# A two-layer diffusion trunk: expert results summed in PSUM, and slot rows read in one piece and transposed by VectorE

## The reference, cut to what matters

```python
comb = jnp.sum(jax.nn.one_hot(eidx, N_EXPERTS) * wsel[..., None], axis=1)
hg = jnp.einsum('td,edf->tef', t, w_gate)
hu = jnp.einsum('td,edf->tef', t, w_up)
act = jax.nn.silu(hg) * hu * comb[:, :, None]
y = jnp.einsum('tef,efd->td', act, w_down)
x = layer_norm(ALPHA * x + g2 * y, ln_w, ln_b)
```

## Time and profile before

| | us |
|---|---|
| median of 3 runs | 1203.97 (1202.0 to 1207.95) |
| the profiled execution | 1201.09 |
| its span | 1199.4 |
| mixture stage of layer 0, first gate matmul to last down | 332.3 to 574.7 |
| first hyena matmul | 613.9 |
| mixture stage of layer 1 | 905.0 to 1164.4 |

### The profile page before, as it was taken

One profiled execution on the slowest core, in us unless ns is written; L12 is line 12 of the kernel. 1 busy time (PEld: TensorE's weight loads), 2 busy tenths in 40 slices (PEclk: granted clock), 3 DMA queues, 4 the chain that ended last, 5 costly groups with the idle time before them and its releaser, 6 DMA issues.

```text
span 1199.4 us, 24149 instructions
## 1 busy us (share of the span) xinstructions
PE 1013.1 (84%) x9499; PEld 561.7 (47%) x9499; DVE 400.3 (33%) x1149; ACT 239.8 (20%) x507; POOL 190.9 (16%) x389
## 2 busy tenths in 40 slices
PE   4899998899769899795679999999978977998564
PEld 2344447654435455453345555455454544555231
DVE  0320115744612222121353533645552221222116
ACT  0401003631411121111131111210141121121102
POOL 0320000300032222122110001002004221222111
PEclk9999999899789999898889999999979998999988
DMA  8998232977589999999892314636765799899984
GB/s 354 324 343 299 95 126 97 350 298 317 222 302 396 388 407 393 397 399 394 305 377 99 140 71 143 243 123 241 292 256 211 270 391 408 337 395 393 394 349 158
DMA packets 76278, 344.62 MB, mean 287 GB/s; under 512 B 8883, under 2 KB 9011, under 8 KB 62900
## 3 DMA queue, kind: packets, MB, share of 16 engines
q1 hardware_dynamic: 54756, 291.40, 62.9%
q0 software_dynamic: 14512, 41.78, 10.2%
q10 hardware_dynamic: 6944, 10.49, 2.5%
HBM read 320.02 MB, written 23.63 MB: 287 GB/s over the span
## 4 chain that ended last, share of the span: by engine, by line
PE 63%; DMA 21%; DVE 10%; ACT 2%; issue 2%; SPq 1%; POOL 0%; POOLq 0%; ACTq 0%; DVEq 0%
PE bank L954 13%; PE bank L743 12%; PE bank L1019 11%; PE bank L961 7%; DMA ring<-in_moe_w_up_dram 7%; PE bank L872 7%; DMA ring<-in_ada_w_dram 3%; DMA ring<-in_moe_w_down_dram 3%; DMA arena<-in_moe_w_up_dram 3%; PE bank L633 3%; DMA ring<-in_ev_w_in_dram 3%; PE bank L1122 1%; PE bank L1098 1%; ACT arena L1409 1%; DVE arena L1531 1%
## 5 line engine op out<-in xcount | busy, mean ns | idle before, releaser
L954 PE MATMUL bank<-ring,arena 128*32 128x256 f32 x2496 | 149.9, 391 | 28.8 <-DMA ring<-in_moe_w_up_dram 25.7
L743 PE MATMUL bank<-ring,arena 128*128 128x512 f32 x336 | 146.7, 598 | 2.5 <-DMA ring<-in_ev_w_in_dram 2.5
L954 PE MATMUL bank<-arena 128*32 128x256 f32 x1792 | 108.1, 395 | 28.3 <-DMA arena<-in_moe_w_up_dram 28.3
L1019 PE MATMUL bank<-arena,ring 128*128 128x384 f32 x384 | 126.3, 492 | 1.9 <-issue 1.9
L1529 DVE TENSOR_TENSOR arena<-arena,bank 128x64 f32<-128x64 f32 x136 | 27.4, 201 | 296.2 <-ACT arena L1409 296.2
L954 PEld LDWEIGHTS bank<-ring,arena 128*32 128x32 f32 x2496 | 83.7, 113 | 88.5 <-issue 41.7
L961 PE MATMUL bank<-ring,arena 128*32 128x256 f32 x1440 | 87.0, 382 | 27.3 <-DVE arena L1531 22.2
L743 PEld LDWEIGHTS bank<-ring,arena 128*128 128x128 f32 x336 | 64.2, 192 | 82.9 <-issue 80.2
L1019 PEld LDWEIGHTS bank<-arena,ring 128*128 128x128 f32 x384 | 73.5, 192 | 54.4 <-issue 5.0
L954 PEld LDWEIGHTS bank<-arena 128*32 128x32 f32 x1792 | 60.3, 114 | 72.0 <-issue 39.4
L872 PE MATMUL bank<-ring,arena 128*128 128x512 f32 x192 | 83.2, 593 | 1.3 <-DVE arena L2096 1.3
(11 more groups left out here) (367 smaller groups left out, 1074.9 us busy)
## 6 DMA issues: line engine op xcount, KB each, us to landing
ring<-in_ada_w_dram SPq DMA_DIRECT2D x24, 2048.0 KB, 13.4
ring<-in_moe_w_down_dram SPq DMA_DIRECT2D x20, 2048.0 KB, 23.5
ring<-in_moe_w_gate_dram SPq DMA_DIRECT2D x18, 2048.0 KB, 24.1
ring<-in_moe_w_up_dram SPq DMA_DIRECT2D x18, 2048.0 KB, 29.4
arena<-in_moe_w_gate_dram SPq DMA_DIRECT2D x14, 2048.0 KB, 26.7
arena<-in_moe_w_up_dram SPq DMA_DIRECT2D x14, 2048.0 KB, 31.9
arena<-in_moe_w_down_dram SPq DMA_DIRECT2D x12, 2048.0 KB, 20.1
ring<-in_ev_w_in_dram SPq DMA_DIRECT2D x7, 2048.0 KB, 19.4
```

The source lines that it names most:

```text
L743: last = pe.matmul(bank[3 * (c % 2) + t], hT[:, k, t * P:(t + 1) * P], slot8(n)[:, k, :], start=k == 0, stop=k == KT - 1)
L954: last = pe.matmul(bank[1][q * BLK:(q + 1) * BLK, 0:HALF], slot_inT[:, k, :], both[:, :, k, q * P:(q + 1) * P], start=k == 0, stop=k == KT ...
L1019: last = pe.matmul(bank[c % 3][:, 0:T], slot8(n)[:, k, (c % 4) * P:(c % 4 + 1) * P], hT[:, k, :], start=k == 0, stop=k == KT - 1)
```

## The change

**Results.** `slot_out` is now 128 partitions by 256: each quarter of the partitions holds a quarter of the 1024 columns for the block's 32 slots. Nothing is stored to DRAM, gathered or joined. Six PSUM banks (`joined`) hold the sums of all 384 tokens through the stage. They are opened with matmuls that write zeros (`begin_sums`). In each block `add_to_tokens` adds the block before it with 12 matmuls: weights are 32 partitions of `sel_w` by 128 tokens, moving data is 32 partitions of `slot_out` by 256 columns, in three groups of four that use the four 32-row groups of the array. `sel_w` holds the router weight where a token owns the slot. VectorE makes it per block from `token_slot` and `token_w`, which TensorE (`along_tokens`) and ScalarE spread over the partitions before the stage. The third group waits until the first has ended. Gate and up stop before their last step until the former block's results and selection are there.

**Rows.** Only block 0 is picked, by 24 matmuls with `h_tok` as weights, directly in channel layout. A block is read as one 128 KB DMA, 4 KB on each of 32 partitions. GpSimd's copy puts it into another order, and VectorE transposes it in four 32x256 pieces. TensorE no longer transposes rows. ScalarE writes `h_tok` unpermuted.

**Around it.** The idle matmuls (`WARM`, `pe_last`) and the scaled identities are gone. Hyena weights wait for no gather. After layer 0, the modulation columns are computed after the totals, and TensorE waits for all three totals before it transposes.

```diff
-            for c in range(WARM):
-                pe.matmul(bank[3], ident, h_tok[:, c % NT, 0:512], start=True, stop=True)
+            pe.wait_ge(weights_rdy, l + 1)
+            for r in range(2):
+                last = along_tokens(bank[1 + r], lambda t: wsel[:, r, t:t + 1])
+            last.then_inc(spread_mm, 1)
+            for b in bank[3:]:
+                begin_sums(b)
...
-            for t in range(NT):
-                for q in range(4):
-                    block, h = divmod(q, 2)
-                    last = pe.matmul(bank[2][q * BLK:(q + 1) * BLK, :], pick[:, t, block * BLK:(block + 1) * BLK],
-                                     h_tok[:, t, h * 512:(h + 1) * 512], start=t == 0, stop=t == NT - 1)
+            for k in range(KT):
+                for t in range(NT):
+                    last = pe.matmul(bank[0][:, k * BLK:(k + 1) * BLK], h_tok[:, t, :].rearrange("p (c k) -> p k c", k=KT)[:, k, :],
+                                     pick[:, t, :], start=t == 0, stop=t == NT - 1)
...
+            def add_to_tokens(turn, closing=False):
+                for t in range(NT):
+                    if t == 2:
+                        pe.wait_ge(S["first_added"], turn)
+                        pe.sem_inc(passed, 1)
+                    for q in range(4):
+                        rows = slice(q * BLK, (q + 1) * BLK)
+                        half = NT * q + t
+                        last = pe.matmul(joined[:, t, q, :], sel_w[rows, t * P:(t + 1) * P], slot_out[rows, :], start=False,
+                                         stop=closing and t > (half ^ 1) % NT)
+                    if t == 0:
+                        last.then_inc(S["first_added"], 1)
+                return last
...
                 for k in range(KT):
+                    if k == KT - 1:
+                        pe.wait_ge(S["evac_dve"], b + 1)
+                        pe.wait_ge(S["evac_act"], b + 1)
+                        pe.wait_ge(S["sel"], b + 1)
                     last = gate_and_up(s, k)
                 last.then_inc(S["gu_mm"], 1)
-                rows_to_channels()
+                add_to_tokens(b + 1)
                 pe.wait_ge(S["act"], b * 2 + 1)
-                pe.wait_ge(S["evac_dve"], b + 1)
-                pe.wait_ge(S["evac_act"], b + 1)
...
+                    pool.tensor_copy(slot_in.rearrange("s (g k i) -> s g k i", g=4, k=KT),
+                                     slot_ahead[k].rearrange("s (g i k) -> s g k i", g=4, k=KT)).then_inc(S["row_rdy"], 1)
+                    pool.wait_ge(S["row_rdy"], pair * 2 + (k + 1))
+                    rows_ahead(pair * 2 + (k + 3), k)
...
-                    for h in range(2):
-                        act.dma_start(slots[bass.ds((pair * 2 + odd) * BLK, BLK), h * 512:(h + 1) * 512],
-                                      slot_out[odd][h * BLK:(h + 1) * BLK, :]).then_inc(S[f"stored{odd}"], 16)
...
+                dve.wait_ge(S["row_rdy"], b + 1)
+                rows_to_channels()
+                dve.wait_ge(S["down_mm"], b + 1)
+                dve.tensor_copy(slot_out[0:2 * BLK, :], bank[1][0:2 * BLK, 0:HALF]).then_inc(S["evac_dve"], 1)
+                for r, o in enumerate((sel_w, sel_w1)):
+                    last = dve.scalar_tensor_tensor(o, token_slot[:, r, :], block_slot, token_w[:, r, :], ALU.is_equal, ALU.mult)
+                last.then_inc(S["sel_step"], 1)
+                dve.wait_ge(S["sel_step"], b * 2 + 1)
+                dve.tensor_tensor(sel_w, sel_w, sel_w1, ALU.add).then_inc(S["sel"], 1)
```

More of the change, by code:

```diff
@@ L385, in trunk_program @@
         idle = tiny(1)
+        block_slot = tiny(1)
+        rows_over = tiny(2)
         warm = tiny(1)
@@ L429, in trunk_program @@
         lnrow_in = sem("lnrow_in")
-        gathered = [sem(f"gathered{t}") for t in range(NT)]
         out_done = sem("out_done")
@@ L569, in pool_moe @@
-            rows_ahead(2, 0)
-            rows_ahead(3, 1)
-            with pool.Fori(1, pairs) as pair:
-                for odd in range(2):
-                    pool.wait_ge(S[f"row_in{odd}"], pair * 32)
-                    pool.wait_ge(S["rowT_mm"], pair * 2 + (odd + 1))
-                    pool.tensor_tensor(idle, wsel[:, 0, 0:1], wsel[:, 0, 0:1], ALU.add)
-                    pool.tensor_copy(slot_in, slot_ahead[odd]).then_inc(S["row_rdy"], 1)
-                    pool.wait_ge(S["row_rdy"], pair * 2 + (odd + 1))
-                    rows_ahead(pair * 2 + (odd + 2), odd)
@@ new lines, in pool_moe @@
+            with pool.Fori(0, pairs) as pair:
+                for k in range(2):
+                    pool.wait_ge(S[f"row_in{k}"], pair * 16 + 16)
+                    pool.wait_ge(S["rowT"], pair * 2 + (k + 1))
+                    pool.tensor_tensor(idle[0:BLK, :], eps_col[0:BLK, :], eps_col[0:BLK, :], ALU.add)
+                    pool.tensor_copy(slot_in.rearrange("s (g k i) -> s g k i", g=4, k=KT),
+                                     slot_ahead[k].rearrange("s (g i k) -> s g k i", g=4, k=KT)).then_inc(S["row_rdy"], 1)
+                    pool.wait_ge(S["row_rdy"], pair * 2 + (k + 1))
+                    rows_ahead(pair * 2 + (k + 3), k)
@@ L584, in pool_moe @@
             if l == 0:
+                pool.wait_ge(S["down_mm"], before_last)
+                pool.tensor_tensor(idle[0:BLK, :], eps_col[0:BLK, :], eps_col[0:BLK, :], ALU.add).then_inc(pool_chain, 1)
+                pool.wait_ge(pool_chain, 2)
                 norm_gate_rows(pool)
-            for odd in range(2):
-                pool.wait_ge(S[f"row_in{odd}"], pairs * 32)
-            pool.wait_ge(S["stored0"], stores * 32 + 32)
-            pool.wait_ge(S["stored1"], odd_stores * 32 + 32)
@@ L590, in pool_moe @@
-            pool.wait_ge(S["rowT"], blocks + 1)
-            pool.tensor_tensor(idle, wsel[:, 0, 0:1], wsel[:, 0, 0:1], ALU.add).then_inc(pool_chain, 1)
-            pool.wait_ge(pool_chain, 2 * l + 3)
-            for t in range(NT):
-                for r in range(2):
-                    pool.indirect_dma_start(picked[:, t, r, :], None, slots[:, :],
-                                            bass.IndirectOffsetOnAxis(ap=idx[:, r * NT + t:r * NT + t + 1], axis=0)).then_inc(gathered[t], 16)
+            for k in range(2):
+                pool.wait_ge(S[f"row_in{k}"], pairs * 16 + 16)
@@ L1419, in act_moe @@
[L1419 to L1425 removed]
+                act.activation(h_tok[:, u // 2, u % 2 * 512:u % 2 * 512 + 512], bank[u], ACT.Copy).then_inc(htok_act, 1)
+            act.wait_ge(spread_mm, 2 * l + 1)
+            for r in range(2):
+                last = act.activation(token_w[:, r, :], bank[1 + r][:, 0:T], ACT.Copy)
```

296 lines of the change are left out of this document (126 added, 170 removed).

## The result

| | before | after |
|---|---|---|
| median | 1205.96 us (4 runs, 1202.0 to 1208.93) | 1232.93 us (4 runs, 1231.77 to 1235.46) |
| span of the profiled execution | 1199.4 | 1230.7 |
| mixture of layer 0, first gate matmul to end of last down | 332.3 to 574.7 | 341.8 to 598.6 |
| first hyena matmul | 613.9 | 633.9 |
| mixture of layer 1, the same | 905.0 to 1164.4 | 935.2 to 1205.9 |

The account below looks back on a forecast made before the run. The mixture was taken as bound by weight transfers, with TensorE some 30 us a layer behind as slack. Terms -19.7 + 4.9 - 9.6 = -24.4 took 1201.09 to 1176.7, median 1179; range 1160 to 1209.

Parts of the forecast that it names:

- The period, TensorE's side: Mixture blocks: six waves of additions on four row groups side by side add 0.6 us, period 6.92 instead of 6.32.
- three quarters: Rival on the additions: four row groups give 3.07 times one's speed; period +0.39 us, +18, 1197 us; chance 0.16.
- The period, VectorE's side: Mixture blocks: VectorE's 3.3 us of added work and GpSimd's copy, doubled to 1.2, lie beside TensorE's 6.92 at no cost.
- a rival with 0.13: Late selection: VectorE's passes can't run beside GpSimd's copy, selection 1.0 us late each block; +46, 1225 us; chance 0.13.
- The slack of the selection: Before gate's last step in each block: selection ready at 6.2, weights load at about 6.45, slack 0.25 us.
- VectorE's own durations: Added work per block: four transposes at 0.38 each, two passes over 384 columns 0.6, a sum 0.54; 3.3 us.
- Lead-in: Before each mixture: spread, zeroing and 48 pick records (5.7 us) delay gate to 336.8 from 332.28, layer 1 by 4.8 us.
- The bound of +11: Upper bound of the lead-in's delay, for weights that load at half pace; the lower bound was +2.
- Behind layer 0: Stores, gathers, joins and hyena weights' wait go; modulation is late next; hyena stage at 594.2 instead of 613.92, -19.7 us.
- The queue gives its time back: Without stores, ScalarE's DMA queue returns 12.7 us a layer, 0.375 a block, where transfers bound.
- End of layer 1: Behind the last down: 12.8 us to the total become 4.2, and totals no longer wait for joins; -9.6 us.
- Layer 1: Mixture: lead-in and longer blocks delay held loads by 9.6, 14 blocks without stores return 5.3, last block 0.6; +4.9 us.

Follow-up runs that it names:

- experiment 1: Changed kernel with GpSimd's row copy waiting for the selection instead of the row transposes: median 1206.42 us, 1.0039 times the kernel before.
- experiment 2: Changed kernel with tokens written in channel order, so the pick's weights have unit stride and GpSimd's copy moves runs of 32: 1196.18 us.
- three_repairs: Changed kernel with copy behind the selection, tokens in channel order and gate rows on ScalarE's queue: median 1188.18 us, 0.9836 times the kernel before.
- experiment 5: Changed kernel with VectorE's two passes reading one SBUF tensor each, every router weight counted as 0.5: 1221.65 us.
- experiment 3: Changed kernel with the norm's gate row loads issued by ScalarE's queue before the last expert, not by GpSimd behind its loop: 1229.78 us.
- experiment 9: `three_repairs` without earlier gate rows, with shorter lead-in and layer 1's stores put back unread: layer 1's last gate 261.9 us after its first, against 255.6 without stores.

## Why the prediction was wrong

The forecast had a span of 1175.0 (1199.4 less 24.4). Measured are 1230.7, 55.7 more. The lengths of the stretches are those of the kernel before with the forecast's terms in them; for the mixture of layer 1 that is 259.4 + 4.9 - 4.8, since the 4.8 of lead-in stand in the row above it:

| stretch | forecast | measured | difference |
|---|---|---|---|
| to the end of the last down of layer 0 | 568.6 | 598.6 | +30.0 |
| from there to the hyena stage | 25.6 | 35.3 | +9.7 |
| hyena stage to the first gate of layer 1 | 295.9 | 301.3 | +5.4 |
| mixture of layer 1 | 259.5 | 270.6 | +11.1 |
| end | 25.4 | 24.9 | -0.5 |

- **The period, TensorE's side: right.** I took 6.92, and it is 6.86 as soon as nothing holds it. All four row groups ran side by side, their six waves in one block of 24 records in 1.61 us. Gate's last wave to down is 0.54 us longer than before, where I had 0.6 with the wait. By the three quarters of the Trainium skill (page "TensorE: Matmul & The Clock Gate", Part 3, "Measured speedup vs the span model") the additions would have cost 0.39 us more; the runs don't show it for this shape (behind the change of shape the waves start 0.22 us apart), and that rival falls.
- **The period, VectorE's side: the step that failed.** "It lies beside TensorE's 6.92, at no cost while the selection is ready", with "doubles to 1.2, and lies beside it too" for GpSimd's copy. The copy took 2.07, since it steps over eight elements, and it holds VectorE's passes. Without one of the two the step would have stood (experiments 1 and 2). Together they cost 0.86 us a period beyond 6.92: some 27 of the 30 us of layer 0 against the forecast (31 periods), and 6 of the 11 of layer 1, by the difference to `three_repairs` (264.3). Repairing them gave back less, 22.0 us in layer 0 (experiment 1). I had this as a rival with 0.13, named the place, and priced it at 1225, with 1.0 us a block and 4.6 us per 0.1. The runs gave 0.86 beyond my period, and in experiment 1 26.3 us of span for 0.92 us of period, 2.9 per 0.1. That the kernel still came out above 1225 is the work of two other misses, the pick and the gate rows below. What I counted against it, transposes that ran undisturbed beside the copy, was true of 128x64 transposes and said nothing of passes, which are held.
- **The slack of the selection: small by 0.2 us.** I had it at 0.25 us, and it was about 0.4: the first pass was held by some 1.35 us (1.96 in most blocks, against 0.61), the period by 0.92. The two shorter passes of experiment 5 add 0.4 to the slack, and its period is 0.52 above 6.86. The 0.3 of hold in experiment 2 cost nothing.
- **VectorE's own durations:** two passes 0.62 each (0.6 taken), the transposes 0.435 (0.38), the sum 0.56 (0.54). Near enough for the sum, but the transposes make the second bound of 6.79.
- **Lead-in: mechanism right, one term mis-sized.** 48 records of the pick were priced at the pace of 24 transposes with unit stride. They took 0.24 each instead of 0.118, 5.8 us a layer. In layer 0 the first gate came 5.0 us later than forecast and block 1 2.6 later (349.6 instead of 347.0). It did not wait for rows read back, as the forecast had it; it followed block 0 after 7.84 us, at the period of the others. With all three repairs it comes at 345.0, 4.6 us earlier, and there it does wait for its rows, by 0.8 us. Layer 1 paid for the pick nearly in full (its first gate came 5.4 us later than forecast against the hyena stage). The bound of +11 held it (9.5 measured in layer 0).
- **Behind layer 0: a cover missed.** "Stores, gathers, joins and the wait in front of the hyena weights go" was right. Asked what is late next, I named the modulation. The gate rows' loads stand on GpSimd behind its row loop, and I put them at nothing. The change moved the loop's last copy behind the last block's row transposes, and with it these loads from 17.6 us before the last down's end to 3.9 us behind it. They cost 8.0 us (experiment 3). With them repaired, the hyena stage starts 26.9 us after the last down, where I had 25.6.
- **The queue gives its time back: right** in experiment 9, but behind an engine that had become the bound it was worth little: DMA share 0.89 and 0.84 in the changed kernel.
- **End of layer 1: right.** 4.2 us from down to the total, and 10.1 gained against 9.6.
- **Layer 1: a rest that is only placed.** Even with all repairs its mixture takes 264.3 us and not 259.5. Up to the first held load it goes as forecast (issued 36.5 us after the first gate; 33.5 before and 3.0 for five longer blocks). The load at 1048.49 before is this one in `three_repairs`:

```profile
1043.02 0.33 SPq L507 DMA_DIRECT2D ring<-in_moe_w_down_dram  x1
```

It comes 149.4 us after the first gate, against 143.5 before and 4.8 forecast, so 1.2 too late. From there to the end of the last down the stage takes 114.9 us against 115.9 before: 1.0 less, where I had 4.7 less (5.3 from the queue and the last block's 0.6). The remaining 3.7 us lie there. This load landed 10.0 us after its issue (7.6 before), and the last block took 9.6 us (8.6 before). Why is open. Experiment 9 says that the stores themselves cost 4.0 in that stretch, so something else took back what the queue gave.

With the three misses cured, the kernel comes near the forecast: 1188 against 1179 in the median, 1184.2 against 1175.0 in the span, half of the difference in layer 1. It is faster than before by 1.6% (1.0 to 2.3), where the forecast had 2.1%.

## What to carry to other kernels

Before work is laid beside other work "at no cost", ask for each pair of instructions that will lie over one another whether the two engines can run at once in exactly these forms. One form that ran undisturbed (a transpose) says nothing of another (a pass over SBUF). Two lateness terms that are harmless alone (a copy of twice the length, and passes that wait for a copy) can add up past the slack, here about 0.4 us, and then the whole of the excess is paid in every period.

Take prices from rows of the same stride: a copy on GpSimd and a weight load of TensorE both doubled with a stride of eight floats. And when a step of a loop is moved behind another wait, look at what the same engine issues behind the loop: it moves as well.

## What the runs showed of the hardware

- GpSimd's copy of 1024 floats on 32 partitions: 1.03 us in runs of 32, 2.07 with a stride of eight. While it runs, VectorE's pass with two SBUF tensors (0.62 alone) and its pass with one (0.41 alone) last until about its end, up to 1.98 and 1.79 us. A copy out of PSUM (0.42), a product with one factor in PSUM (0.18 to 0.22), and transposes of 128x64 in 32x32 pieces (0.24) keep their times.
- Float32 weight loads of 128x128 with a stride of 32 bytes: one matmul each 0.24 us at either level of the granted clock, against 0.12 with unit stride. In layer 1 the profile shows TensorE 100% busy in the pick, and still the granted clock fell from 1.00 to 0.50 during it.
- Four row groups of the array with 32 rows each kept the pace of four column groups, 0.22 us a wave: six waves and the change of shape behind them took 1.53 us.
